# Second attention of a two-block fp32 transformer kernel: one score bank for each of the four heads, turned probabilities through three banks, inverse sums spread ahead of the last turning

## The reference, cut to what matters

```
for each block of 128 queries (start = 0, 128, 256, 384):
    score = sum over 8 index heads of relu(qi . ki) * wi, causal
    sel   = the 128 best keys of each query
    for each of 4 key/value groups, 4 query heads each:
        logits = q . k * 64**-0.5, with -1e30 where a key is not selected
        p      = softmax(logits)
        o      = p @ v
```

## Time and profile before

| what | value |
|---|---|
| median of 3 runs | 1755.95 us (1755.88 to 1760.2) |
| the profiled execution, its own time | 1760.43 us |
| span of the profiled execution | 1758.6 us |
| PE busy | 1682.4 us, 96% of the span |
| DVE busy | 1018.0 us, 58% |
| ACT busy | 703.0 us, 40% |
| granted TensorE clock, mean | 0.98 |

### The profile page before, as it was taken

One profiled execution on the slowest core, in us unless ns is written; L12 is line 12 of the kernel. 1 busy time (PEld: TensorE's weight loads), 2 busy tenths in 40 slices (PEclk: granted clock), 3 DMA queues, 4 the chain that ended last, 5 costly groups with the idle time before them and its releaser, 6 DMA issues.

```text
span 1758.6 us, 23023 instructions
## 1 busy us (share of the span) xinstructions
PE 1682.4 (96%) x7756; PEld 1338.5 (76%) x7756; DVE 1018.0 (58%) x2010; ACT 703.0 (40%) x1331; POOL 77.0 (4%) x62
## 2 busy tenths in 40 slices
PE   6998999999998998889999999999999899999999
PEld 5777677777887676547788888887888788888887
DVE  7788766666456688844655564467454533333344
ACT  5363666663344244763433322324223333332322
POOL 0020000000000064110000000000000000000000
PEclk9998999999998998999899999999999999999999
DMA  6453344444331121003355554353333233333333
GB/s 238 156 154 113 109 136 171 156 149 138 95 96 60 48 72 49 1 2 95 120 191 192 191 197 139 108 192 95 95 96 96 72 104 100 96 95 96 96 96 108
DMA packets 56775, 202.82 MB, mean 115 GB/s; under 512 B 6576, under 2 KB 6704, under 8 KB 56560
## 3 DMA queue, kind: packets, MB, share of 16 engines
q1 hardware_dynamic: 56688, 201.68, 35.2%
HBM read 198.38 MB, written 2.10 MB: 114 GB/s over the span
## 4 chain that ended last, share of the span: by engine, by line
PE 88%; DVE 8%; ACT 3%; issue 2%; DMA 0%; DVEq 0%; POOLq 0%; POOL 0%; ACTq 0%
PE bank L479 25%; PE bank L480 24%; PE bank L481 24%; PE bank L582 2%; PE bank L632 2%; PE bank L522 1%; PE bank L603 1%; PE bank L523 1%; DVE WORK L1934 1%; DVE SM L1933 1%; DVE W_lo L1418 1%; PE bank L525 1%; PE bank L528 1%; PE bank L502 1%; PE bank L504 1%
## 5 line engine op out<-in xcount | busy, mean ns | idle before, releaser
L479 PE MATMUL bank<-H_hi,W_hi 128*128 128x512 f32 x1336 | 534.7, 400 | 3.2 <-DVE W_lo L1418 2.0
L480 PE MATMUL bank<-H_lo,W_hi 128*128 128x512 f32 x1336 | 521.7, 391 | 0.0
L481 PE MATMUL bank<-H_hi,W_lo 128*128 128x512 f32 x1336 | 521.4, 390 | 0.0
L1418 DVE TENSOR_TENSOR W_lo<-RAW,W_hi 128x512 fp32r<-128x512 f32 x538 | 351.5, 692 | 199.1 <-ACT W_hi L907 185.3
L907 ACT ACTIVATE W_hi<-RAW 128x512 fp32r<-128x512 f32 x538 | 317.0, 625 | 281.0 <-PE bank L481 229.6
L479 PEld LDWEIGHTS bank<-H_hi,W_hi 128*128 128x128 f32 x1336 | 251.6, 188 | 74.8 <-issue 20.5
L480 PEld LDWEIGHTS bank<-H_lo,W_hi 128*128 128x128 f32 x1336 | 251.7, 188 | 54.3 <-issue 4.6
L481 PEld LDWEIGHTS bank<-H_hi,W_lo 128*128 128x128 f32 x1336 | 251.5, 188 | 53.6
L481 PE MATMUL bank<-A_hi,W_lo 128*128 128x512 f32 x352 | 137.0, 389 | 0.0
L480 PE MATMUL bank<-A_lo,W_hi 128*128 128x512 f32 x352 | 136.9, 389 | 0.0
L479 PE MATMUL bank<-A_hi,W_hi 128*128 128x512 f32 x352 | 136.9, 389 | 0.0
(11 more groups left out here) (263 smaller groups left out, 2049.5 us busy)
## 6 DMA issues: line engine op xcount, KB each, us to landing
RAW<-weights SPq DMA_DIRECT2D x269, 512.0 KB, 3.7
AW<-ada SPq DMA_DIRECT2D x100, 512.0 KB, 3.7
X<-x_t SPq DMA_DIRECT2D x4, 512.0 KB, 6.5
y_t<-X SPq DMA_DIRECT2D x8, 256.0 KB, 2.0
LW<-lru_w SPq DMA_DIRECT2D x1, 1024.0 KB, 12.4
QX<-QR SPq DMA_DIRECT2D x40, 16.0 KB
CROW<-crow SPq DMA_DIRECT2D x1, 512.0 KB, 10.4
ROPE<-rope SPq DMA_DIRECT2D x1, 512.0 KB, 13.2
```

What stands on the lines that cost most here:

```text
L479: pe.matmul(dst, wh, ch(hi, k), start=(k == 0), stop=False)
L480: pe.matmul(dst, wh, ch(lo, k), start=False, stop=False)
L481: mm = pe.matmul(dst, wl, ch(hi, k), start=False, stop=(k == chunks - 1))
L1418: dve.tensor_tensor(W_lo[:, w], RAW[:, c:c + HALF], W_hi[:, w], ALU.subtract).then_inc(lo_done, 1)
```

## The change

The four heads of a step get a score bank each (2, 7, 5, 3), and `qk(s, h)` waits for `score(s - 1, h)` in place of the score three heads back. Bank 3 is therefore no longer free for the fourth key chunk: turned probabilities go through banks 0, 1 and 4, the fourth chunk into bank 0 again, behind a wait for the copy of the first chunk. `spread(s)` moves from behind `turn_probs(s)` into it: ahead of the only chunk of a one-chunk step, ahead of the second of two, ahead of the third of three or four. Before the loop, `rot2(13)` goes to bank 1 in place of 3, so the waits for banks 0 and 1 move ahead of it, and a wait for the rope of tile 12 stands ahead of `qk(16, (3,))`.

```diff
--- before.py
+++ after.py
@@ -575,14 +575,26 @@
                         if s and h == 0:
                             pe.wait_ge(ttr_done, 4 * s)
                     else:
-                        dst = ps[QK_BANKS[m % 3]][:, 0:w]
-                        pe.wait_ge(ttr_done, 64 + m - 2)
+                        dst = ps[QK_BANKS[h]][:, 0:w]
+                        if s > 16:
+                            pe.wait_ge(ttr_done, 64 + m - 3)
                     rows = slice(64 * half, 64 * half + 64)
                     k0 = KD_AT(g, half) + keys[0] * P
                     mm = pe.matmul(dst, Q[rows, chunk * S + n * P:chunk * S + (n + 1) * P],
                                    KD[rows, k0:k0 + w],
                                    start=True, stop=True)
                     mm.then_inc(qk_mm, 1)
+
+            def spread(s):
+
+                pe.wait_ge(recip_done, s - 15)
+                if s > 16:
+                    pe.wait_ge(yt_out, s - 16)
+                for h in range(4):
+                    odd, c = h % 2, (s % 2) * 24 + 16 + h
+                    mm = pe.matmul(ps[6][odd * HD:(odd + 1) * HD, (2 + h // 2) * P:(3 + h // 2) * P],
+                                   SM[:, c:c + 1].to_broadcast([P, HD]), cs("ident"), start=True, stop=True)
+                mm.then_inc(spread_mm, 1)
 
             def turn_probs(s):
 
@@ -597,22 +609,15 @@
                 if s:
                     pe.wait_ge(pt_out, PT_COUNT[s])
                 for c in range(len(keys)):
+                    if c == min(2, len(keys) - 1) and s >= 16:
+                        spread(s)
+                    if c == 3:
+                        pe.wait_ge(pt_out, PT_COUNT[s] + 1)
                     for h in range(4):
                         src = (s % 2) * 4 * width + h * w + c * P
                         to = (h % 2 * 2 + h // 2) * P
-                        mm = pe.transpose(ps[banks[c]][:, to:to + P], SB[:, src:src + P], cs("ident"))
+                        mm = pe.transpose(ps[banks[c % len(banks)]][:, to:to + P], SB[:, src:src + P], cs("ident"))
                     mm.then_inc(pt_mm, 1)
-
-            def spread(s):
-
-                pe.wait_ge(recip_done, s - 15)
-                if s > 16:
-                    pe.wait_ge(yt_out, s - 16)
-                for h in range(4):
-                    odd, c = h % 2, (s % 2) * 24 + 16 + h
-                    mm = pe.matmul(ps[6][odd * HD:(odd + 1) * HD, (2 + h // 2) * P:(3 + h // 2) * P],
-                                   SM[:, c:c + 1].to_broadcast([P, HD]), cs("ident"), start=True, stop=True)
-                mm.then_inc(spread_mm, 1)
 
             def pv(s):
 
@@ -715,7 +720,7 @@
 
                 pe.wait_ge(head_in, i + 1)
                 pe.wait_ge(rope_done, 10 + i)
-                pe.matmul(ps[3][:], cs("rot2"), ch(QN, (i + 1) % 3), start=True, stop=True).then_inc(rot_mm, 1)
+                pe.matmul(ps[1 if i == 13 else 3][:], cs("rot2"), ch(QN, (i + 1) % 3), start=True, stop=True).then_inc(rot_mm, 1)
 
             def index(n, k):
 
@@ -829,13 +834,14 @@
                     pe.wait_ge(x_new, 16)
                 linear(Tile(T_QKV2 + 9 + c), H_hi, H_lo, between=in_q(c))
 
+            pe.wait_ge(rope_done, 10 + 13)
             qk(16, (3,))
             qk(17, (0, 1))
+            pe.wait_ge(bank_free[0], Tile(T_AO2 + T_AO2 % 2).uses)
+            pe.wait_ge(bank_free[1], Tile(T_AO2 + 1 - T_AO2 % 2).uses)
             rot2(13)
             query_columns(7)
             qk(17, (2, 3))
-            pe.wait_ge(bank_free[0], Tile(T_AO2 + T_AO2 % 2).uses)
-            pe.wait_ge(bank_free[1], Tile(T_AO2 + 1 - T_AO2 % 2).uses)
             pe.wait_ge(v_done, 4)
             for s in range(16, 32):
                 if s == 17:
@@ -843,10 +849,9 @@
                     pe.wait_ge(rope_done, 10 + 14)
                 if s > 16:
                     pv(s - 1)
-                turn_probs(s)
                 if s == 16:
                     pe.wait_ge(head_var, 5)
-                spread(s)
+                turn_probs(s)
                 if s < 30:
                     qk(s + 2)
             pv(31)
@@ -1048,7 +1053,7 @@
                     act.wait_ge(pv_mm, s)
                 for c in range(len(keys)):
                     act.wait_ge(pt_mm, PT_COUNT[s] + c + 1)
-                    act.copy(ch(PT, c), ps[banks[c]][:]).then_inc(pt_out, 1)
+                    act.copy(ch(PT, c), ps[banks[c % len(banks)]][:]).then_inc(pt_out, 1)
 
             def y_region(t, s):
                 g, n, _ = STEPS[s]
@@ -1875,7 +1880,7 @@
             def rope2_out(i):
                 dve.wait_ge(rot_mm, i + 1)
                 dst = ch(QI, i) if i < 4 else (ch(QR, i - 4) if i < 6 else ch(Q, i - 6))
-                turned(i, ch(QN, (i + 1) % 3) if i < 6 else None, ps[3][:], dst)
+                turned(i, ch(QN, (i + 1) % 3) if i < 6 else None, ps[1 if i == 13 else 3][:], dst)
                 dve.sem_inc(rope_done, 1)
 
             def index_keys_normed():
@@ -2009,12 +2014,11 @@
                 g, n, keys = STEPS[s]
                 w = len(keys) * P
                 m = (s % 2) * 24
-                i = 4 * (s - 16) + h
                 if h == 0 and s > 17:
                     dve.wait_ge(pt_mm, PT_COUNT[s - 1])
                 dve.wait_ge(qk_mm, 4 * s + h + 1)
                 a = (s % 2) * 4 * S + h * w
-                dve.tensor_tensor_reduce(out=SB2[:, a:a + w], in0=ps[QK_BANKS[i % 3]][:, 0:w], in1=BIAS[:, n * S:n * S + w],
+                dve.tensor_tensor_reduce(out=SB2[:, a:a + w], in0=ps[QK_BANKS[h]][:, 0:w], in1=BIAS[:, n * S:n * S + w],
                                          scale=1.0, scalar=-3e38, op0=ALU.add, op1=ALU.max,
                                          accum_out=SM[:, m + h:m + h + 1]).then_inc(ttr_done, 1)
 
@@ -2203,8 +2207,8 @@
 TWO_PI_PARTS.append(_rest)
 
 
-QK_BANKS = (2, 7, 5)
-PT_BANKS = ((4, 5), (0, 1, 4, 3))
+QK_BANKS = (2, 7, 5, 3)
+PT_BANKS = ((4, 5), (0, 1, 4))
 PAIR_BANK = 3
 U_ORDER = (1, 0, 2, 3, 4, 5, 6, 7)
 Q_PARTS = ((0, 32), (32, 24), (56, 8))
```

## The result

The changed kernel takes 1761.52 us, median of 20 runs (1755.23 to 1764.58). The kernel before has 1757.43 us over 20 runs, and the ratio is 1.0022 (95% interval 1.0015 to 1.0030): 3.9 us slower, 2.6 to 5.3. The profiled execution took 1763.44 us with a span of 1761.7.

The account below looks back on a forecast made before the run. In the stretch without linears, DVE bounds steps with top-key rounds, PE those after. Terms +0.3, -4.7, +0.2, +3.75, -0.7 give -1.15 us; one clock fall (+1.5) makes +0.35, on median 1755.95: 1756.3 us, range 1751.3 to 1761.5.

Parts of the forecast that it names:

- the fourth rival: Steps 21 to 26: the edit doesn't decouple, gain only 2 of 4.7 us; +3.05 in all, 1759.0 us; chance 0.15.
- The bank for each head: Steps 21 to 26: DVE limited by its own work, no longer idling for `pv` and `qk`; gain 4.7 us.
- the sign: In the changed trace, DVE's idle time between 714 and 754 us is under 1 us.
- with nearly nothing to spare: Steps 21 to 26: PE needs 5.95 us, some 0.1 of it overlapping, against DVE's period of about 5.8.
- The fourth chunk's copy wait: Four-chunk steps: waiting for the first chunk's copy costs 2.1 us at `qk(30)` and 1.65 us at `qk(31)`.
- My terms for steps 27 to 31: Step 27 +0.2 us, steps 28 and 29 +3.75 for the copy wait, steps 30 and 31 -0.7 from earlier copies.
- I count one fall that hits `qk(30)`: PE's clock falls once in the last four steps, costing 1.5 us and turning -1.15 into +0.35 us.
- The second rival: Steps 28 to 31: the clock stays low throughout; +10.5 us, 1766.5 us; chance 0.10.
- The one-chunk steps: Steps 16 to 19, spread ahead of turning: loss of 0.3 us at start of step 21 (gain 2.5 to loss 1).
- The third rival: The clock stays high in steps 16 to 19, 2.5 us more won; -3.65 us, 1752.3 us; chance 0.14.
- PE's work: Steps 28 to 31: about 14 us of PE work on the path, with each `qk` taken as 3.1 us.
- the circle: Four-chunk steps: `qk`, scores, exponentials, ACT's copies, fourth chunk, next `qk`; 9.09 us a round against 7.0 and 7.44 before.

Follow-up runs that it names:

- e7: The change with three idle-filling fp32 matmuls ahead of the first spread, in step 16: 1758.07 us, ratio 0.9997 to the kernel before.
- e5: The change with two idle-filling fp32 matmuls ahead of the copy wait in steps 28, 29 and 30: 1757.79 us, ratio 0.9996 to the kernel before.
- e4: The change with bank 3 for fourth-head scores through step 29 and fourth chunks from step 28, no copy wait: 1753.91 us, ratio 0.9978 to the kernel before.
- e1: The change with the spread back behind the turning in steps 16 to 27: 1754.95 us, ratio 0.9984 to the kernel before.
- e12: The change with the spread back behind the turning in steps 16 to 19 only: 1757.72 us, ratio 0.9996 to the kernel before.
- e10: The change with the spread back behind the turning in step 16 alone: 1761.05 us, ratio 1.0019 to the kernel before.
- e6: The change with bank 3 serving both uses, no copy wait, and the spread behind the turning in steps 16 to 27: 1751.41 us, ratio 0.9955.
- e9: The kernel before with one idle-filling fp32 matmul ahead of its first spread: 1755.13 us, ratio 0.9987 to the kernel before.
- e3: The kernel before with the fourth chunk's copy wait, and the spread moved in steps 28 to 31 only; three score banks: 1761.09 us, ratio 1.0020.

## Why the prediction was right and wrong

The median, 1761.52 us, lies at the very upper end of the range (1761.5), 0.02 us past it. Against the kernel before, measured at 1757.43 us in the same runs, it is 3.9 us slower where I forecast +0.35. The ratio of 1.0022 is within the 0.3% to which I gave 0.80. That the range reaches so far is in part luck: its upper end was the fourth rival, which didn't come, with 2.5 us for a second and third fall. And I put my sum on a median of three runs, 1755.95 us; over 20 runs it was 1.5 us higher.

- *The bank for each head: right.* Steps 21 to 26 gained 4.43 us, forecast 4.7. Every version with four score banks has 35.38 to 35.40 us there, whatever else it does. DVE idles 1.46 us in that stretch, 0.3 of it for `pv`; I had put the sign at under 1. That PE keeps pace "with nearly nothing to spare" was wrong, see the last point.
- *The fourth chunk's copy wait: right in mechanism and size.* At the full clock the last stretch is made up of 1.75 us from `y_scaled(26)` to `qk(29)` and 9.01 to `qk(30)` (both e7), 9.02 to `qk(31)` and 18.32 to the first linear (both e5), in all 38.1, 3.5 over before. My terms for steps 27 to 31 sum to 0.2 + 3.75 - 0.7 = 3.25; one by one they came out at 0.3, 3.6 and -0.4.
- *"I count one fall that hits `qk(30)`": the step that failed.* The clock fell four times in the last stretch, in both profiles of the change, 13.8 and 14.0 us at the low clock: once behind the 1.89 us wait for `y_scaled(26)` and three times behind the copy wait. 43.28 - 38.1 = 5.2 us for four, 1.3 each; I had priced one well (1.5) and counted it once. So the falls beyond the one counted are 3.7 of the 3.9 us by which the last stretch went past my 3.25 + 1.5. The first stretch took 1.1 us off that and the middle added 0.3, so the profile is at +3.38 where I had +0.35. e5 shows the three falls at the copy as a cause: filling the idle time takes 3.94 us off the stretch and 3.7 off the kernel.
- *The second rival*, a low clock throughout steps 28 to 31 at +10.5 us, didn't come: PE regained the full clock ahead of each new wait. I had read the rule of the Trainium skill on cycling through PSUM banks with short gaps ("TensorE: Matmul & The Clock Gate", section "A second HAM failure mode: psum-queue depth-cycling") as a low clock throughout. It tells of a swing between the two levels, and the trace of the change agrees with that from 748 us on. That of e4 doesn't: it goes round banks as well, with stops of 1.90 us and less between its matmul groups, and its last stretch is at 1.00.
- *The one-chunk steps.* I forecast +0.3 against the kernel before, and it was -0.84 and -0.77. But I costed the moved spread as nearly free, while e1 and e12 show that it takes 2.9 us there: 1.3 to 1.8 by its order (e7) and the rest by the clock. That the term came out near was luck, since two errors hid each other: without the moved spread the change is 3.8 us under the kernel before in this stretch (e12), at the full clock, where the kernel before spent 10.5 us at the low one. The third rival, a clock that stays high there, didn't come: the change spent 7.0 us at the low one. In step 27 I had +0.2; `y_scaled(26)` to `(27)` was 6.97 against 6.21, +0.76, with a fall of the clock in it, and 5.89 without (e7).
- *"PE's work" in the four-chunk steps was misread.* I took the 3.15 us of a `qk` row as the work of four heads that would stay. It is 1.99 with four score banks. The row of 3.15 hides that the fourth head started behind the third, when the first score was done, and not beside it. PE itself hardly stood still in it: the two parts sum to 3.10. The weight loads show the wait (the load of the fourth head), and in step 26, where the stop is long enough to split the row, three heads take 1.98 us and the fourth alone 1.12 (PE and PEld of the kernel before):

```profile
764.76 0.29 PEld L582 LDWEIGHTS bank<-KD,Q 64*128 64x128 f32 x2 [0.87 <-DVE SM L2017]
```

```profile
747.70 1.98 PE L582 MATMUL bank<-KD,Q 64*128 64x512 f32 x6
751.18 1.12 PE L582 MATMUL bank<-KD,Q 64*128 64x512 f32 x2 [1.49 <-DVE SM L2017]
```

  So PE has more room in the changed kernel than I gave it and its idle time in the circle is longer (2.33 and 1.90 us, forecast 2.1 and 1.65). That this puts the clock more in danger is argued, not shown.

How much of the moved spread's cost in the timed runs is clock and how much order stays a rough split: e10 shows that a single profile can fall either way. Why the clock falls behind one wait and not behind another of the same length stays open.

## What to carry to other kernels

A buffer given to one queue is taken from another: work out the circle that closes at the place it left, and ask for how long each side really needs it. Here bank 3 serves both, since scores and chunks want it in different steps, and the version that does that is 0.2% faster than the kernel before with the spread moved (e4), and 0.4% with it back behind the turning in steps 16 to 27 (e6). Put a wait behind the independent work of an in-order queue and not ahead of it, and price PE's idle time twice, once as time and once as the clock of the work behind it.

## What was unexpected of the hardware

- More work made the kernel faster: two idle-filling matmuls in each of three waits of 1.9 to 2.3 us saved 3.7 us (e5), and one in a wait of 1.6 us some 2.4 us (e9).
- In the last stretch of the change, idle times of PE of 1.9 and 2.3 us at the copy were each followed by a fall to 1.2 GHz. One of 1.43 us in e3 and one of 1.42 us in e6 were not, nor were those of 1.90 us in e4 and of 1.90 and 2.23 us in e7, while one of 1.33 us in the kernel before was (at 718.29 us). So the length alone doesn't decide.
- Equal rows don't give an equal clock: the PE rows of e6 and e10 agree to 0.03 us from 640 to 692.3 us, and then they ran 18 us at 1.00 and at 0.53.
- The fourth head of a `qk` cost almost nothing once it didn't have to wait: four heads 1.56 us, three 1.55, and a fourth on its own 0.91 more.
